# One kernel, one address: the start of the shared SBUF pool moved by 128 bytes

## The chip, the cores and the metric

The kernel runs on one core of a Trainium2 chip. The metric is the device time of one execution in microseconds. The kernel before was timed in three runs: 1452.28, 1457.98 and 1458.26 us, median 1457.98 us. A smaller number is better.

## The reference

The program computes three transformer-like layers on 256 tokens of width 1024, in float32. The first layer has a recurrent branch and an attention branch side by side; the next two have feed-forward, a mixer, a second feed-forward and a gated embedding.

```python
def reference(x, c, positions, ..., p_2, positions_2, norm_g_2, ffn1_w_in_2, ...):
    x = first_block(x, c, positions, ...)     # modulated norm, RG-LRU branch + windowed attention
    return second_block(x, p_2, positions_2, ...)

# second_block, for each of two layers i:
h = h + 0.5 * rmsnorm(swiglu(rmsnorm(h, g[0]), ffn1_w_in[i], ffn1_w_out[i]), g[1])
mix = even_mixer(...) if i % 2 == 0 else odd_mixer(...)   # HGRN2 + window attention, or retention
h = h + rmsnorm(mix, g[3])
h = h + 0.5 * rmsnorm(swiglu(rmsnorm(h, g[4]), ffn2_w_in[i], ffn2_w_out[i]), g[5])
gate = sigmoid(h @ ple_w_gate[i])
h = h + rmsnorm(gate * (p[i] @ ple_w_proj[i]), g[6])
```

`swiglu` is `(silu(x @ w_gate) * (x @ w_up)) @ w_out` with a hidden width of 2816.

## The kernel before

All weights come from HBM as "units" of 1 MB, 2048 float32 numbers on each of 128 partitions. Queue SP loads them into a ring of four (`raw`). For each unit ScalarE makes a rounded copy `whi` (L418) and VectorE the remainder `wlo = raw - whi` (L1181). The activations are split in the same way into a high and a low part. A product is then three matmuls in float32r (L2011 to L2013): high by `whi`, high by `wlo`, low by `whi`. The activations are the stationary operand (the loaded weights of the array, 128x128), the unit is the moving one (512 columns as a rule).

The 256 tokens are two tiles `t` of 128. In each stage TensorE goes through the units of the stage for t = 0 and then for t = 1; `acc[t]` in PSUM takes the sums; ScalarE and VectorE evacuate them, TensorE turns the results (L2064) and the other two engines split them again for the next stage. The order on each engine is written out by hand; semaphores hold it together. Nothing in it depends on an address.

SBUF is laid out by hand too. `sb` puts a tensor at the running offset `base[0]`, rounded up to 32 bytes (L124 to L128); `placed` puts one at a given offset (L121). Offsets are the same on all partitions. First comes what lives all the time: `raw`, `whi`, `wlo`, `h`, `xn`, `feed_hi`, `feed_lo`, gains, small tensors, `setup` and the constants. The constants of the odd layer (`decay`, `onorm_c`, L188 to L189) lie over those of the even layer and end at byte 153824. Behind them begins the pool, at `pool_at` (L190): four overlapping layouts, one each for the first layer (L193), the feed-forwards with `hid_hi` and `hid_lo` (L231), the even mixer (L241) and the odd mixer (L275). One tensor of 8 KB, `pp1` (with `fT`, `ff` and `pT0` over it), is hung from the upper end of SBUF instead (L232).

The offsets of the kernel before, in bytes and modulo 256, in the program as it is built:

| tensors | offset | mod 256 |
|---|---|---|
| `raw`, `whi`, `wlo` | 1152, 33920, 66688 | 128 |
| `h`, `xn`, `feed_hi`, `feed_lo`, `gpre`, `gpost` | 99456 to 136320 | 128 |
| `ident` (in `setup`) | 145120 | 224 |
| `decay`, `onorm_c`, `bias_b`, `mask_a`, `reset_a` | 145632 on | 224 |
| `ident_r`, `bias_r` | 150304, 150816 | 32 |
| the pool's start: `qT`, `qcT`, `feed2_hi`, `ang`, `pp0` | 153984 | 128 |
| `kT`, `hid_hi`, `mod_more`, `v1`, `mod_part`, `sz`, `hid_lo`, `hid`, `ymix`, `vc`, `sgc`, `att_c`, `red` | in the pool | 128 |
| `trn` | in the pool | 0 |
| `xc`, `rg`, `ig`, `w_ax`, `s1`, `gate_part`, `ones` | in the pool | 192 |
| `pp1`, `fT`, `ff`, `pT0` | 221056 on | 128 |

`cos_t` is at 0 and `sin_t` at 128 modulo 256; both are outside the pool.

Of the kernel before, what the change touches and what calls it, by code (L numbers as in the profile page):

```python
# [26 lines left out]
P = 128  # L27
# [22 lines left out]
C_HEADS, C_DK, C_DV = 4, 256, 512  # L50
# [63 lines left out]
def build(nc, io):  # L114
    with ExitStack() as ctx:
# [5 lines left out]
        def placed(name, shape, dtype, at):  # L121
            return nc.alloc_sbuf_tensor_at(name, shape, dtype, offset=at)
# [56 lines left out]
        const_at = base[0]  # L179
# [7 lines left out]
        bias_r = sb("bias_r", [P, 3 * P], F32R)  # L187
        decay = placed("decay", [P, C_HEADS, 3 * P], F32, const_at)  # L188
        onorm_c = placed("onorm_c", [P, C_DV], F32, const_at + 4 * C_HEADS * 3 * P)  # L189
        pool_at = (const_at + 4 * (C_HEADS * 3 * P + C_DV) + 127) // 256 * 256 + P  # L190


        base[0] = pool_at  # L193
# [2540 lines left out]
```

## Time and profile before

| | |
|---|---|
| median of three runs | 1457.98 us |
| the profiled execution's own time | 1452.28 us |
| its span | 1450.3 us |
| TensorE busy (matmul) | 1413.8 us, 97% |
| VectorE, ScalarE busy | 870.2 us, 60%; 717.3 us, 49% |
| granted TensorE clock, mean | 0.998 |
| DMA, mean | 188 GB/s |

The span is what the profiler saw of the program's instructions, and lies 2.0 us under the execution's own time. A matmul's end in the trace is modelled, so the mean duration of one (some 390 ns) is longer than the distance from one start to the next; the pace of TensorE is read from the starts in the timeline.

### The profile page before, as it was taken

How to read it: one execution, taken by the hardware profiler on the slowest of the kernel's cores; microseconds unless marked ns; L12 is line 12 of the kernel's file. 1: busy time of each engine (PE TensorE's matmuls, PEld its weight loads, DVE VectorE, ACT ScalarE, POOL GpSimd, SP SyncE). 2: the span in 40 equal slices, each digit the busy share in tenths (PEclk: the TensorE clock that was granted, in tenths of full speed). 3: DMA queues.
4: the chain of work that ended last, by engine and by line, in shares of the span. 5: the costliest groups of instructions: out<-in, count | busy, mean ns of one | idle time of the engine just before them, and what ended most of it. 6: DMA issues, size and time to landing. Idle time of an engine off the chain costs nothing.

```text
span 1450.3 us, 17117 instructions
## 1 busy us (share of the span) xinstructions
PE 1413.8 (97%) x6598; PEld 1169.5 (81%) x6598; DVE 870.2 (60%) x810; ACT 717.3 (49%) x728; POOL 80.1 (6%) x91
## 2 busy tenths in 40 slices
PE   7999999999999999999999999999999999999997
PEld 6787887777888887878888878888888878888886
DVE  7768686685554575765554575554674545654536
ACT  5674667454443456654443463543443545453434
POOL 0000000010000100110000020000202101100001
PEclk9999999999999999999999999999999999999999
DMA  9745645465646373336454655554554543644551
GB/s 394 288 147 213 221 135 185 149 221 207 230 157 219 127 258 117 145 131 231 151 200 172 228 207 203 185 194 180 195 203 146 200 148 120 243 176 172 192 186 44
DMA packets 40380, 272.51 MB, mean 188 GB/s; under 512 B 4609, under 2 KB 5505, under 8 KB 8706
## 3 DMA queue, kind: packets, MB, share of 16 engines
q1 hardware_dynamic: 36864, 261.65, 49.6%
q10 hardware_dynamic: 3458, 10.04, 2.2%
q8 instruction: 42, 0.69, 0.2%
q14 instruction: 16, 0.13, 0.0%
HBM read 270.62 MB, written 1.05 MB: 187 GB/s over the span
## 4 chain that ended last, share of the span: by engine, by line
PE 86%; DVE 9%; ACT 3%; issue 2%; POOL 0%; DMA 0%; DVEq 0%; POOLq 0%; ACTq 0%
PE acc L2011 26%; PE acc L2013 26%; PE acc L2012 26%; DVE wlo L1181 3%; PE turn L2064 3%; DVE xn L1235 1%; DVE h L1251 1%; PE turn L2213 0%; DVE feed_lo L1219 0%; PE aux L2548 0%; ACT whi L418 0%; PE aux L2139 0%; DVE mod_part L1331 0%; DVE xn L1244 0%; DVE red L1311 0%
## 5 line engine op out<-in xcount | busy, mean ns | idle before, releaser
L1181 DVE TENSOR_TENSOR wlo<-raw,whi 128x2048 fp32r<-128x2048 f32 x233 | 533.1, 2298 | 268.7 <-ACT whi L418 268.4
L2011 PE MATMUL acc<-whi,feed_hi 128*128 128x512 f32 (+1 forms) x1496 | 595.5, 398 | 9.1 <-DVE wlo L1181 7.6
L2013 PE MATMUL acc<-whi,feed_lo 128*128 128x512 f32 (+1 forms) x1496 | 583.1, 390 | 0.0
L2012 PE MATMUL acc<-wlo,feed_hi 128*128 128x512 f32 (+1 forms) x1496 | 582.6, 389 | 0.0
L418 ACT ACTIVATE whi<-raw 128x2048 fp32r<-128x2048 f32 x233 | 445.6, 1917 | 254.7 <-PE acc L2013 243.4
L2011 PEld LDWEIGHTS acc<-whi,feed_hi 128*128 128x128 f32 x1496 | 282.0, 188 | 68.9 <-DVE wlo L1181 9.6
L2013 PEld LDWEIGHTS acc<-whi,feed_lo 128*128 128x128 f32 x1496 | 281.8, 188 | 59.8
L2012 PEld LDWEIGHTS acc<-wlo,feed_hi 128*128 128x128 f32 x1496 | 282.2, 189 | 55.9 <-issue 1.2
L2011 PE MATMUL acc<-whi,hid_hi 128*128 128x512 f32 x352 | 138.0, 392 | 0.0
L2013 PE MATMUL acc<-whi,hid_lo 128*128 128x512 f32 x352 | 137.1, 389 | 0.0
L2012 PE MATMUL acc<-wlo,hid_hi 128*128 128x512 f32 x352 | 137.0, 389 | 0.0
L2013 PEld LDWEIGHTS acc<-whi,hid_lo 128*128 128x128 f32 x352 | 66.1, 188 | 13.7
L2012 PEld LDWEIGHTS acc<-wlo,hid_hi 128*128 128x128 f32 x352 | 66.1, 188 | 13.4
L2011 PEld LDWEIGHTS acc<-whi,hid_hi 128*128 128x128 f32 x352 | 66.1, 188 | 13.3
L675 ACT ACTIVATE hid_hi<-turn 128x512 f32 (+2 forms) x48 | 26.4, 549 | 99.3 <-PE turn L2064 99.3
L1654 DVE TENSOR_TENSOR hid_lo<-turn,hid_hi 128x512 f32 (+2 forms) x48 | 30.8, 642 | 71.5 <-ACT hid_hi L675 71.5
L1081 POOL TENSOR_SCALAR ms<-ss 128x1 f32<-128x1 f32 x18 | 14.3, 795 | 1062.6 <-ACT xn L438 1042.9
L1645 DVE SCALAR_TENSOR_TENSOR hid<-acc,pre_rs,sgl 128x512 f32<-128x512 f32 (+1 forms) x48 | 33.8, 703 | 46.2 <-ACT sgl L668 42.3
L1219 DVE TENSOR_TENSOR feed_lo<-turn,feed_hi 128x512 fp32r<-128x512 f32 x48 | 31.0, 686 | 35.2 <-ACT feed_hi L460 35.1
L460 ACT ACTIVATE feed_hi<-turn 128x512 fp32r<-128x512 f32 x48 | 26.2, 593 | 51.4 <-PE turn L2064 51.4
L668 ACT ACTIVATE sgl<-acc,pre_rs 128x512 f32<-128x512 f32 x40 | 27.1, 678 | 37.7 <-PE acc L2013 37.6
L2064 PE MATMUL turn<-setup,xn 128*128 128x128 f32 x250 | 34.8, 279 | 6.1 <-DVE xn L1235 6.1
(325 smaller groups left out, 862.9 us busy)
## 6 DMA issues: line engine op xcount, KB each, us to landing
raw<-in_units SPq DMA_DIRECT2D x237, 1024.0 KB, 4.9
mod_raw<-in_units SPq DMA_DIRECT2D x6, 1024.0 KB, 11.6
gpost<-in_norm_g ACTq DMA_DIRECT2D x8, 512.0 KB, 4.5
gpre<-in_norm_g ACTq DMA_DIRECT2D x6, 512.0 KB, 6.1
mod_more<-in_units SPq DMA_DIRECT2D x2, 1024.0 KB, 23.8
h<-in_x SPq DMA_DIRECT2D x2, 512.0 KB, 8.8
w_ax<-in_w_ax SPq DMA_DIRECT2D x1, 1024.0 KB, 25.7
bgate<-in_b_gate SPq DMA_DIRECT2D x1, 1024.0 KB, 27.1
```

The source lines that it names most:

```text
L418: act.activation(whi[:, u % RING, :], raw[:, u % RING, :], ACT.Copy).then_inc(hi_ready, 1)
L460: act.activation(dst[:, 4 * i:4 * i + 4, lanes(t)], turn[:, b, :].rearrange("p (c s) -> p c s", c=4), ACT.Copy).then_inc(fed_hi, 1)
L668: act.activation(sgl[:, t, :, :], acc[t][:, :].rearrange("p (i n) -> p i n", i=2)[:, :, 0:256], ACT.Silu, scale=pre_rs[:, t:t + 1]).then_i ...
L675: act.activation(dst, turn[:, b, 0:P * count].rearrange("p (c s) -> p c s", c=count), ACT.Copy).then_inc(fed_hi, 1)
L1181: dve.tensor_tensor(wlo[:, u % RING, :], raw[:, u % RING, :], whi[:, u % RING, :].bitcast(F32), ALU.subtract).then_inc(lo_ready, 1)
L1219: dve.tensor_tensor(dst[part], turn[:, b, :].rearrange("p (c s) -> p c s", c=4), hi_part[part].bitcast(F32), ALU.subtract).then_inc(moved[ ...
L1645: dve.scalar_tensor_tensor(hid[:, t, 0:tiles, :], up, pre_rs[:, t:t + 1], sgl[:, t, 0:tiles, :], ALU.mult, ALU.mult)\
L1654: dve.tensor_tensor(hid_lo[:, at, lanes(t)], turn[:, b, 0:P * count].rearrange("p (c s) -> p c s", c=count), hid_hi[:, at, lanes(t)].bitca ...
L2011: pe.matmul(out, xh, wh, start=first, stop=False)
L2012: pe.matmul(out, xh, wl, start=False, stop=False)
L2013: return pe.matmul(out, xl, wh, start=False, stop=last)
L2064: last = pe.transpose(turn[:, b, P * i:P * i + P], part, ident[:, :])
```

## The change

The expression for the start of the pool is another one.

```diff
--- before.py
+++ after.py
@@ -187,7 +187,7 @@
         bias_r = sb("bias_r", [P, 3 * P], F32R)
         decay = placed("decay", [P, C_HEADS, 3 * P], F32, const_at)
         onorm_c = placed("onorm_c", [P, C_DV], F32, const_at + 4 * C_HEADS * 3 * P)
-        pool_at = (const_at + 4 * (C_HEADS * 3 * P + C_DV) + 127) // 256 * 256 + P
+        pool_at = (const_at + 4 * (C_HEADS * 3 * P + C_DV) + 127) // 128 * 128
 
 
         base[0] = pool_at
```

With the constants' end at 153824, the old expression gives 153951 // 256 * 256 + 128 = 153984, the new one 153951 // 128 * 128 = 153856. Each tensor of the pool lies 128 bytes lower than before: those at 128 modulo 256 come to 0, those at 192 to 64, `trn` from 0 to 128. `pp1` and its overlays stay, and so does all that stands ahead of the pool. No instruction is added, removed or moved on any engine or queue, and no shape changes.

## Rows read from the trace of the kernel before

**Rows 1.** The page: busy time by engine, and the chain that ended last

```profile
PE 1413.8 (97%) x6598; PEld 1169.5 (81%) x6598; DVE 870.2 (60%) x810; ACT 717.3 (49%) x728; POOL 80.1 (6%) x91
PE 86%; DVE 9%; ACT 3%; issue 2%; POOL 0%; DMA 0%; DVEq 0%; POOLq 0%; ACTq 0%
PE acc L2011 26%; PE acc L2013 26%; PE acc L2012 26%; DVE wlo L1181 3%; PE turn L2064 3%; DVE xn L1235 1%; DVE h L1251 1%; PE turn L2213 0%; DVE feed_lo L1219 0%; PE aux L2548 0%; ACT whi L418 0%; PE aux L2139 0%; DVE mod_part L1331 0%; DVE xn L1244 0%; DVE red L1311 0%
```

**Rows 2.** Waits of TensorE: us in total, times, longest us

```profile
PE aux L2128 <- DMA mod_raw<-in_units: 8.3, 1, 8.3
PE acc L2011 <- DVE wlo L1181: 7.6, 6, 2.6
PE turn L2064 <- DVE xn L1235: 6.1, 7, 1.8
PE aux L2139 <- DVE mod_part L1334: 2.5, 1, 2.5
```

**Rows 3.** Timeline of TensorE in the second feed-forward matrix: start us, us, instruction

```profile
469.65 0.39 PE L2012 MATMUL acc<-wlo,hid_hi 128*128 128x512 f32 x1
...
472.37 0.39 PE L2012 MATMUL acc<-wlo,hid_hi 128*128 128x512 f32 x1
```

**Rows 4.** The same where `feed_hi` is the stationary operand

```profile
603.71 0.39 PE L2011 MATMUL acc<-whi,feed_hi 128*128 128x512 f32 x1
...
605.53 0.40 PE L2013 MATMUL acc<-whi,feed_lo 128*128 128x512 f32 x1
```

**Rows 5.** The same at the narrow unit of the even mixer, 256 columns

```profile
514.63 0.28 PE L2012 MATMUL acc<-wlo,feed_hi 128*128 128x256 f32 x1
...
515.35 0.28 PE L2012 MATMUL acc<-wlo,feed_hi 128*128 128x256 f32 x1
```

**Rows 6.** The same early in a deep group, with a longer step

```profile
451.26 0.40 PE L2013 MATMUL acc<-whi,hid_lo 128*128 128x512 f32 x1
451.50 0.39 PE L2011 MATMUL acc<-whi,hid_hi 128*128 128x512 f32 x1
451.72 0.40 PE L2012 MATMUL acc<-wlo,hid_hi 128*128 128x512 f32 x1
```

**Rows 7.** Groups by form, TensorE: busy us, mean ns of one, idle before

```profile
L2011 PE MATMUL acc<-whi,hid_hi 128*128 128x512 f32 x352 | 138.0, 392 | 0.0
L2213 PE MATMUL turn<-xc,w_ax 128*128 128x256 f32 x32 | 7.6, 381 | 0.4 <-DVE qT L1208 0.4
L2226 PE MATMUL aux<-kT,qT 128*128 128x256 f32 x16 | 4.8, 380 | 0.0
L2548 PE MATMUL aux<-vc,att_c 128*128 128x512 f32 x16 | 7.9, 593 | 0.0
L2273 PE MATMUL aux<-gate_part,ones 128*128 128x512 f32 x4 | 1.9, 592 | 0.0
...
L2012 PEld LDWEIGHTS acc<-wlo,hid_hi 128*128 128x128 f32 x352 | 66.1, 188 | 13.4
```

**Rows 8.** Groups by form, VectorE

```profile
L1307 DVE TENSOR_SCALAR trn<-trn 128x352 f32<-128x352 f32 x2 | 0.7, 344 | 0.1
L1315 DVE TENSOR_SCALAR red<-red 128x352 f32<-128x352 f32 x1 | 0.3, 344 | 0.0
L1535 DVE TENSOR_TENSOR sz<-sz,xc 128x1024 f32<-128x1024 f32 x2 | 2.5, 1226 | 0.3
L1505 DVE TENSOR_TENSOR ig<-ig,xc 128x1024 f32<-128x1024 f32 x2 | 2.4, 1216 | 0.0
L1461 DVE TENSOR_TENSOR h<-h,xn 128x1024 f32<-128x1024 f32 x2 | 2.5, 1226 | 0.1
```

**Rows 9.** The start: DMA issues (KB each, us to landing), ScalarE's wait, one window

```profile
mod_more<-in_units SPq DMA_DIRECT2D x2, 1024.0 KB, 23.8
ACT whi L418 <- DMA raw<-in_units: 7.4, 3, 5.3
20.00:40.00 20.00, 20.00 (x93) 17.77 (x93) 14.87 (x15) 12.57 (x15) 0.00 (x0) 1.00 1.01 419
```

## The prediction

> **What bounds the kernel now.** I read the busy shares first, then the chain that ended last, then TensorE's waits, and then the starts of its matmuls one by one. TensorE is busy for 97% of the span, and the chain runs through it for 86% [rows 1]; 78% of the span is the three lines of the split product. What TensorE waits for is short: the four largest entries are 8.3, 7.6, 6.1 and 2.5 us, 24.5 us together [rows 2], and the two of them that don't belong to the start are 13.7 us. So there are two ways in which a change of address can move the time: another pace of the matmuls, or another duration of one of the few instructions of VectorE and ScalarE (and of the loads at the start) that the chain passes through.
>
> The pace is read from starts. In the second feed-forward matrix twelve steps lie between 469.65 and 472.37 us [rows 3], which is 226.7 ns a matmul. With `feed_hi` as the stationary operand eight steps lie between 603.71 and 605.53 [rows 4], 227.5 ns. With 256 columns in place of 512, six steps take 0.72 us [rows 5], 120 ns. The difference, 106.7 ns for 256 columns, is 0.417 ns a column, so 512 columns are 213.3 ns, and 13.3 ns in each matmul are a fixed part. TensorE keeps this pace for as long as it isn't made to wait: it is the bound, and nothing in it looks like a queue for SBUF.
>
> **The change, part by part.** No instruction comes, goes or changes its place or its shape, so there is no removed or added work to sum. What changes is the address of operands. By arithmetic the pool goes from 153984 to 153856, a move of 128 bytes, and from 128 to 0 modulo 256. It is a real move, so the case "the new expression gives the same address" is out. The constants below it end at 153824 and the nearest tensor above, `pp1`, stays, so nothing overlaps anew and no semaphore gets another meaning. I take the operands engine by engine.
>
> 1. TensorE. The moving operand of the split product (`whi`, `wlo`) stays where it is. The stationary one moves in three places: `hid_hi` and `hid_lo` in the four feed-forwards, 3 x 352 = 1056 matmuls (one of the three groups of 352 stands in [rows 7]; the other two have the same count); `feed2_hi` and `feed2_lo` in one group of the odd mixer, 4 units by 2 tiles by 12 matmuls = 96 by the code; `pT1` in one projection of the embedding, 24 (one unit, 2 tiles by 4 blocks by 3). That is 1176 matmuls. The trace has no matmul with an operand at 0 modulo 256, so their new pace isn't shown; what it shows are the neighbours. At 192 modulo 256 (`xc`, `w_ax`) a matmul of 256 columns is 381 ns, at 128 (`kT`, `qT`) 380 ns; with `gate_part` and `ones`, both at 192, one of 512 columns is 592 ns, with `vc` and `att_c`, at 128, 593 ns [rows 7]. Two different addresses of this kind differ by 1 ns in 380 to 590. I take 0 for the move. The bounds: above, the longer step that sometimes appears even now, 0.24 us between 451.26 and 451.50 against 0.22 to 0.23 around it [rows 6]; with the hundredths of the view that is up to some 9 ns over the usual step, and if all 1176 matmuls had it the sum is 1176 x 9 = 10.6 us. Below, the fixed part: if the loading of an aligned operand hid all of the 13.3 ns, the gain were 1176 x 13.3 = 15.7 us.
>
> 2. VectorE and ScalarE. Here the trace does have both alignments. The same operation on 352 elements takes 344 ns where `trn` is at 0 modulo 256 and 344 ns where `red` is at 128 [rows 8]. An addition or product of 1024 elements takes 1226 ns with one operand at 128 and the other at 192, 1226 ns with both at 128 (`h`, `xn`), and 1216 ns with both at 192. So the largest difference is 10 ns in 1226, 0.8%, and it is not tied to the pool's edge. The chain has 9% of VectorE and 3% of ScalarE [rows 1]; less the 3% for `wlo`, whose operands don't move, 9% of 1450.3 us are 131 us. With all of it changed by 0.8% that is 1.0 us in either direction. I take 0. Off the chain these engines have 40% and 51% of the span to spare, so there is cover for any such difference; if it were gone, this 1.0 us is what it costs.
>
> 3. DMA. The transfers into the pool all come at the start, apart from one `pT` load and a one-row bias. Between 20 and 40 us the DMA share is 1.01 at 419 GB/s, and ScalarE waits 7.4 us for units in this part of the program [rows 9]. So the start does depend on transfers, and `mod_more`, two transfers of 1 MB, stands in the queue ahead of the units that ScalarE waits for. At 419 GB/s the two are 2 x 1.05 MB / 419 = 5.0 us of the queue. The ring's own rows of the same size go to addresses at 128 modulo 256 now, and will still; no row of this trace has a transfer of that size to an address at 0, so I bound it by a tenth of these 5.0 us either way, 0.5 us, and take 0.
>
> A rule of the Trainium skill bears on this last term. The page "DMA: Bandwidth & Descriptors", section "How a descriptor splits into AXI transactions", says that a transfer is cut into pieces of 256 B which must begin at a multiple of 256, so that a misaligned one pays for a further piece. By it, read as holding for the destination too, a row of 8192 B of `mod_more` needs 33 pieces now and 32 after the change, 3% less: an estimate by that page of 0.15 us gained in 5.0 us. No run here has shown it yet, and the ring's 237 loads wouldn't gain, since they stay where they are.
>
> The sum is 0 us, with -15.7 - 1.0 - 0.5 and 10.6 + 1.0 + 0.5 as its outer bounds. Against the profiled execution's own 1452.28 us (its span 1450.3 and 2.0 around it) that is 1452.3 again. The two other runs of the kernel before are at 1457.98 and 1458.26, so the profiled one is the fast end of the scatter; the mean of the three is 1456.2 and their median 1458.0. A median of some runs of an unchanged kernel should fall between them: I forecast 1457.0 us.
>
> **The rivals.**
>
> Slower: the two reads of TensorE get into each other's way. Now the stationary and the moving operand both begin at 128 modulo 256; after the change the stationary one of 1176 matmuls begins at 0 and the moving one still at 128. If SBUF served reads that begin in the same half of 256 bytes better than others, each of these matmuls would get a longer step. Its place is the feed-forwards; its price by [rows 6] is up to 9 ns each, 10.6 us, so 1467.6 us. It decides by more than 0.5% from 6.2 ns a matmul on (7.3 us / 1176). For it: steps of 0.24 us do occur in the trace with no change of work. Against it: in [rows 7] neither `w_ax` nor `ones` at another alignment costs anything. The Trainium skill, page "SBUF — State Buffer", section "Who interferes with whom", speaks against it as well: TensorE has one read port for the moving operand and an independent one for the loading, and never waits. The steady 226.7 ns agree with that, but a run with the two operands apart isn't among the rows.
>
> Faster: the aligned stationary operand loads faster, and a part of the fixed 13.3 ns goes. The full price is 15.7 us, which gives 1441.3; half of it, 7.8 us, gives 1449.2. For it: there is a fixed part, and nothing in the trace has an operand at 0, so it can't be excluded. Against it: at 192 and at 128 modulo 256 it is the same, and a load takes 188 ns [rows 7] against a step of 227, beside the matmul before, so it seems to be covered.
>
> Also possible is a shift of the evacuations or of the start (points 2 and 3), by at most 1.5 us together in either direction. It stays within the forecast, whatever its sign.
>
> **How the numbers follow.** About 0.5%, 7.3 us, is what a measurement of this kernel can tell from no change. I give the forecast (no change, the small shifts included) 0.64, the slower case 0.20, and the faster one 0.16. The last two aren't smaller because the one alignment that the change brings is just the one that TensorE's rows don't show. The scatter of the runs before, 6 us, is under the half per cent. The likeliest case alone would span 1451 to 1461. The range reaches to the slower case's full price at 1468, and towards the faster one to 1445, something over its half price: 1445 to 1468. Faster 0.16, same 0.64, slower 0.20.
>
> **What would show it right or wrong.** Right: in the profile after, the starts in the second feed-forward matrix are again 227 ns apart, as are those with `feed_hi`; VectorE's groups of the same form agree within 10 ns; the waits of TensorE are the same few, within 2 us. The slower rival shows as a step over 227 ns with `hid_hi` and `hid_lo` and not with `feed_hi`; the faster one as a step under 227 there. The start is judged by ScalarE's wait for units, 7.4 us now. The forecast is wrong if the medians of both kernels, run side by side, lie over 0.5% apart, and wrong in its reasons if any group whose operands moved has another mean while the total happens to agree.

## The result, and the profile after

The kernel after takes 1463.82 us (median of 12 runs, 1459.42 to 1465.99) against 1455.43 us for the kernel before in the same comparison (12 runs, 1452.28 to 1458.26). The ratio is 1.0055, with a 95% interval of 1.0044 to 1.0066: slower, by 8 us, through an address alone. Not one instruction is another.

The page of the profile after, busy time and then the chain, against [rows 1]:

```profile
span 1462.6 us, 17117 instructions
PE 1426.6 (98%) x6598; PEld 1175.2 (80%) x6598; DVE 870.2 (59%) x810; ACT 717.7 (49%) x728; POOL 79.2 (5%) x91
PE 87%; DVE 9%; ACT 3%; issue 1%; POOL 0%; DMA 0%; DVEq 0%; POOLq 0%; ACTq 0%
```

The span is 12.3 us longer and TensorE is busy 12.8 us longer; VectorE and ScalarE have the same busy time to within 0.4 us. The waits of TensorE after (us in total, times, longest) are those of [rows 2]:

```profile
PE aux L2128 <- DMA mod_raw<-in_units: 8.0, 1, 8.0
PE acc L2011 <- DVE wlo L1181: 7.3, 5, 2.6
PE turn L2064 <- DVE xn L1235: 6.2, 7, 1.8
PE aux L2139 <- DVE mod_part L1334: 2.8, 1, 2.8
```

So the time is not in a wait that the profile knows. It is in the pace, the distance from the start of one matmul to the start of the next (a step). In the second matrix of the first feed-forward 180 matmuls with `hid_hi` and `hid_lo` stand in a row. I take the last 168 of them, 167 steps, in both kernels. Timeline of before (start us, us, instruction; `...` stands for lines left out):

```profile
461.95 0.39 PE L2011 MATMUL acc<-whi,hid_hi 128*128 128x512 f32 x1
...
499.80 0.39 PE L2013 MATMUL acc<-whi,hid_lo 128*128 128x512 f32 x1
```

and of after:

```profile
464.23 0.39 PE L2011 MATMUL acc<-whi,hid_hi 128*128 128x512 f32 x1
...
480.26 0.40 PE L2011 MATMUL acc<-whi,hid_hi 128*128 128x512 f32 x1
480.50 0.39 PE L2012 MATMUL acc<-wlo,hid_hi 128*128 128x512 f32 x1
...
503.04 0.39 PE L2013 MATMUL acc<-whi,hid_lo 128*128 128x512 f32 x1
```

37.85 us / 167 = 226.7 ns before, 38.81 / 167 = 232.4 ns after. The three other feed-forwards give the same two numbers to 0.02 ns, worked out from the unrounded starts. Before, every step is 226 or 227 ns; after, they run 228, 230, 233, 241, 232, 231, 232 and round again, whether VectorE and ScalarE are busy at the time or not. The duration that the profile prints for a matmul shows it less exactly: this group went from 392 ns [rows 7] to 398, the two others with `hid` from 389 to 394, and that with `whi` and `feed_hi`, of which at most 32 in 1480 have an operand that moved, from 399 to 401.

```profile
L2011 PE MATMUL acc<-whi,hid_hi 128*128 128x512 f32 x352 | 140.0, 398 | 0.0
L2213 PE MATMUL turn<-xc,w_ax 128*128 128x256 f32 x32 | 7.6, 381 | 0.4 <-DVE qT L1208 0.4
L2548 PE MATMUL aux<-vc,att_c 128*128 128x512 f32 x16 | 7.9, 593 | 0.0
L2273 PE MATMUL aux<-gate_part,ones 128*128 128x512 f32 x4 | 1.9, 592 | 0.0
```

The other rows of that group moved too, from 192 to 64 or from 128 to 0 modulo 256, and are unchanged to the nanosecond.

Summed over all starts, the steps that follow a `hid` matmul are 5.8 us longer than before, those of the 96 with `feed2` 0.55 us, and those of the 24 with `pT1` 0.12 us: 6.5 us. The remaining 5.8 us between the two spans (that it is the same number is chance) lie in stretches in which one of the two executions was granted the lower clock. Three stretches of after, us, busy times, then granted clock, DMA share, GB/s:

```profile
328.40:331.90 3.50, 3.50 (x11) 2.88 (x11) 1.38 (x2) 1.20 (x2) 0.00 (x0) 0.51 0.72 186
632.20:635.70 3.50, 3.17 (x10) 2.68 (x11) 1.66 (x3) 2.25 (x5) 0.21 (x2) 0.51 0.02 5
860.90:867.80 6.90, 6.02 (x14) 4.75 (x15) 2.03 (x3) 0.48 (x2) 1.43 (x2) 0.51 0.87 345
```

and the place of the first in before:

```profile
327.90:331.40 3.50, 3.50 (x20) 2.87 (x19) 1.55 (x3) 1.20 (x2) 0.07 (x1) 1.00 0.54 166
```

In the three the clock is at its lower level, 1.2 GHz, and the first holds 11 matmuls where the same 3.5 us of before hold 20. These stretches come and go from one execution to the next in both kernels, so I compare executions of equal mean clock, over all that are on record for the two kernels. The median span is 1457.8 us against 1450.5 at the clock 0.998 (2 executions of after, 6 of before), 1460.1 against 1453.9 at 0.996 (5 and 20), and 1462.0 against 1455.3 at 0.994 (4 and 8): 7.3, 6.2 and 6.7 us. That is the change, and it is the 6.5 us counted in the steps above to within 0.8 us.

The other 2 us or so of the 8.4 between the medians go with a lower clock: 11 of the 23 executions of after are at 0.993 or 0.992, and none of the 40 of before. Whether the address does that isn't shown. The kernel with the ring moved, below, has the same longer steps and ran at 0.994 to 0.996, in four executions.

### The profile page after: what moved, and what is told of

Same layout as the page of the kernel before. It is cut to its first block, busy times and chain, and to the rows that moved or that the text cites. A ratio compares the mean times of both kernels' runs of the same rounds, so it can differ in the third digit from the quotient of the medians.

```text
span 1462.6 us, 17117 instructions
## 1 busy us (share of the span) xinstructions
PE 1426.6 (98%) x6598; PEld 1175.2 (80%) x6598; DVE 870.2 (59%) x810; ACT 717.7 (49%) x728; POOL 79.2 (5%) x91
## 4 chain that ended last, share of the span: by engine, by line
PE 87%; DVE 9%; ACT 3%; issue 1%; POOL 0%; DMA 0%; DVEq 0%; POOLq 0%; ACTq 0%
PE acc L2011 26%; PE acc L2013 26%; PE acc L2012 26%; PE turn L2064 4%; DVE wlo L1181 3%; DVE xn L1235 1%; PE turn L2213 0%; DVE feed_lo L1219 0%; PE aux L2548 0%; DVE h L1251 0%; PE aux L2139 0%; DVE mod_part L1331 0%; DVE red L1311 0%; DVE xn L1244 0%; ACT whi L418 0%
## 5 line engine op out<-in xcount | busy, mean ns | idle before, releaser
L1081 POOL TENSOR_SCALAR ms<-ss 128x1 f32<-128x1 f32 x18 | 13.3, 740 | 1074.6 <-ACT xn L438 1054.7
## 6 DMA issues: line engine op xcount, KB each, us to landing
mod_more<-in_units SPq DMA_DIRECT2D x2, 1024.0 KB, 23.5
```

## The experiments

I had one theory to test from here, A: a matmul's step gets longer where the stationary operand and the moving one stand at different places modulo some power of two. The rivals stand in each expectation. Two operands are called in step where they start at the same place modulo 256, and out of step otherwise. All kernels start from the kernel before, and the cuts of code are shortened. Where a table gives the step, it is that over the last 168 matmuls of the stage, as above.

**Put `hid` back, and move everything else in the pool.**

```diff
-        pool_at = (const_at + 4 * (C_HEADS * 3 * P + C_DV) + 127) // 256 * 256 + P
+        pool_at = 153856
-        hid_hi = sb("hid_hi", ...); hid_lo = sb("hid_lo", ...)
+        # both placed 128 bytes higher than sb would
```

> The pool starts at 153856 as after the change, but hid_hi and hid_lo alone are put back to 128 modulo 256. Theory A (a matmul step gets longer where the stationary operand and the moving one begin in different halves of 256 bytes): the steps with hid_hi and hid_lo are 227 ns again, 6 us of the 8 come back, and the median is at most 0.1% over that of before; the 96 matmuls with feed2 and the 24 with pT1 keep their longer step, 0.6 us. Rival B (the loss is in the granted clock and in other tensors of the pool): hid's steps are 227 ns but the time stays about 0.5% over before. Rival C (the trace's longer steps come from something that follows the pool's start as such): hid's steps stay at 232.9 ns.

1457.25 us (11 runs), ratio to before 1.0006 (0.9997 to 1.0015). Timeline of this kernel:

```profile
464.46 0.39 PE L2017 MATMUL acc<-whi,hid_hi 128*128 128x512 f32 x1
...
502.31 0.39 PE L2019 MATMUL acc<-whi,hid_lo 128*128 128x512 f32 x1
```

226.7 ns again. The two `hid` tensors carry the loss: all other tensors of the pool together are worth at most 0.15%, the upper end of the interval, and that includes the 0.6 us of `feed2` and `pT1`. Rival B, the clock or the rest of the pool, and rival C fall.

**Move the ring instead of the pool.**

```diff
-        base = [(nc.sbuf_usable_end - nc.sbuf_bytes_remaining + 31) // 32 * 32]
+        base = [(nc.sbuf_usable_end - nc.sbuf_bytes_remaining + 31) // 32 * 32 + 128]
...
+        pool_at = 153984     # the value that before has
```

> All tensors ahead of the pool (raw, whi, wlo, h, xn, feed_hi, feed_lo, constants) move up by 128 bytes to 0 modulo 256, and the pool stays at 153984, 128 modulo 256. Theory A, as a matter of the distance between the two operands: hid's steps are 232.9 ns, feed's 227, time 0.5% over before, as after the change. Rival A2, as a matter of the stationary operand's own address (0 modulo 256 is bad): hid's steps are 227, those of feed_hi and feed_lo 232.9, 4392 x 5.7 ns = 25 us more than before, 1.7%. Rival A3 (a moving operand at 0 modulo 256 is bad or good by itself): all steps change alike.

1462.04 us (4 runs), ratio 1.0043 (1.0027 to 1.0058).

```profile
462.56 0.39 PE L2011 MATMUL acc<-whi,hid_hi 128*128 128x512 f32 x1
...
501.37 0.39 PE L2013 MATMUL acc<-whi,hid_lo 128*128 128x512 f32 x1
```

`hid` hasn't moved here; `whi` and `wlo` have, and the step is 232.4 ns, while those with `feed_hi` and `feed_lo`, which moved along with the ring, keep 227. It is the distance between the operands, not the address of either.

**Ring and pool at 0 modulo 256.** The same with `pool_at = 154112`. `pp1` and what lies over it, hung from the upper end, stay at 128.

> Everything ahead of the pool at 0 modulo 256 (moved up by 128) and the pool at 154112, 0 modulo 256 as well. Distance theory: hid's and feed's steps are all 227 ns and the time is that of before, ratio 0.998 to 1.002. Rival (an operand of TensorE at 0 modulo 256 costs or gains by itself): steps other than 227 in both groups.

1456.04 us (10 runs), ratio 1.0001 (0.9991 to 1.0012).

```profile
463.04 0.39 PE L2011 MATMUL acc<-whi,hid_hi 128*128 128x512 f32 x1
...
500.89 0.39 PE L2013 MATMUL acc<-whi,hid_lo 128*128 128x512 f32 x1
```

37.85 us again, so 226.7 ns, as in the three other stages; 156 matmuls with `feed_hi` and `feed_lo` in a row step at 227.3 ns here and before. This closes the square: ring and pool at (128, 128) and (0, 0) are alike, (128, 0) and (0, 128) are both slower.

**Put the other operand out of step.** `base[0] += 128` ahead of `feed_hi`, `pool_at = 153984`.

> feed_hi and feed_lo, and the gains and constants behind them, move up by 128 bytes; raw, whi, wlo and the pool stay. The suspected cost is put on the other 4392 matmuls of the split product. Theory A: their steps are 232 to 233 ns in place of 227, 4392 x 5.7 = 25 us more, a ratio of 1.017 to before, less where TensorE waits anyway; hid's steps stay at 227. Rival (the effect belongs to hid's stage: no turns in between, addresses in the high part of SBUF): feed's steps stay at 227 and the time is that of before.

1473.23 us (4 runs), ratio 1.0114 (1.0098 to 1.0129). A stage of 156 matmuls with `feed_hi` and `feed_lo`, before:

```profile
1111.80 0.48 PE L2011 MATMUL acc<-whi,feed_hi 128*128 128x512 f32 x1
...
1147.03 0.39 PE L2013 MATMUL acc<-whi,feed_lo 128*128 128x512 f32 x1
```

and here:

```profile
1130.51 0.48 PE L2012 MATMUL acc<-whi,feed_hi 128*128 128x512 f32 x1
...
1166.61 0.40 PE L2014 MATMUL acc<-whi,feed_lo 128*128 128x512 f32 x1
```

35.23 / 155 = 227.3 ns against 36.10 / 155 = 232.9, while the steps with `hid` are at 226.7 again. The effect follows the operands, in this stage as in that of `hid`. Its size was expected at 25 us and came to 17 us between the medians. At equal mean clock the spans are 20 us apart at 0.998 (1470.8 against 1450.5) and 17 at 0.997 (1469.4 against 1452.3), from one or two executions each. Over the whole kernel the mean step with `feed` rose from some 227.6 to 232.8 ns, 5.2 and not 5.7, which makes 23 us. A part of the rest is in TensorE's waits, which are shorter in this profile: 6.1 us in place of 7.6 for `wlo` and 5.0 in place of 6.1 for `xn`, with 9.5 in place of 8.3 for `mod_raw` against them.

One group of `feed` shows no loss: the 48 matmuls of 256 columns in the even mixer. Here, out of step,

```profile
523.83 0.28 PE L2012 MATMUL acc<-whi,feed_hi 128*128 128x256 f32 x1
...
526.57 0.28 PE L2014 MATMUL acc<-whi,feed_lo 128*128 128x256 f32 x1
```

23 steps take 2.74 us, 119 ns each, against 120 before [rows 5]. So the 5.7 ns are shown for 512 columns alone.

**Which load, and which distance.** From here each feed-forward has its own pair of `hid` tensors at its own offset, four distances in one run:

```diff
+        hid_his = [placed(f"hid_hi{k}", [P, FF_CHUNKS, SEQ], F32R, hid_at + d)
+                   for k, d in enumerate((128, 0, 64, 32))]
+        hid_los = [placed(f"hid_lo{k}", [P, FF_CHUNKS, SEQ], F32R, hid_at + hid_size + d)
+                   for k, d in enumerate((0, 128, 64, 32))]
```

> The pool as before; in each of the four feed-forwards hid_hi and hid_lo lie somewhere else: in the first hid_hi is 128 bytes off and hid_lo in place, in the second the other way round, in the third both 64 bytes off, in the fourth both 32. Theory A, each load paying for its own distance to the moving operand: the mean step over a stage of 180 is 226.7 + 2/3 x 5.7 = 230.5 ns in the first and 228.6 in the second; in the third and fourth it says nothing yet: equal to 232.9 if any distance but a multiple of 256 costs, 227 if only the half of 256 bytes counts and 32 and 64 leave both in one half, in between if it grows with distance. Rival (one disturbed step upsets all that follow): 232.9 in the first and in the second.

```profile
465.50 0.39 PE L2017 MATMUL acc<-whi,hid_hi 128*128 128x512 f32 x1
...
504.46 0.39 PE L2019 MATMUL acc<-whi,hid_lo 128*128 128x512 f32 x1
...
780.30 0.39 PE L2017 MATMUL acc<-whi,hid_hi 128*128 128x512 f32 x1
...
818.90 0.40 PE L2019 MATMUL acc<-whi,hid_lo 128*128 128x512 f32 x1
...
997.55 0.39 PE L2017 MATMUL acc<-whi,hid_hi 128*128 128x512 f32 x1
...
1036.51 0.39 PE L2019 MATMUL acc<-whi,hid_lo 128*128 128x512 f32 x1
```

One run, 1463.61 us. 38.96, 38.60 and 38.96 us for 167 steps: 233.3, 231.1 and 233.3 ns, and 233.3 in the fourth. Two misses. A load out of step does not simply pay its third: `hid_hi` alone out of step (233.3) is worse than both (232.4), and `hid_lo` alone costs 4.4 ns, over two thirds of the full price. And the half of 256 bytes isn't the unit: 32 bytes off cost as much as 64.

**More distances.** (96, 192, 224, 256), then (160, 288, 384, 512), the same for both tensors.

> Both hid tensors off by 96, 192, 224 and 256 bytes in the four feed-forwards; all else as before. If only a distance of a multiple of 256 is in step: 233 to 234 ns in the first three stages and 227 in the last. If only the order matters (the load a little behind the moving operand costs, a little ahead doesn't): 227 at 224 as well. If it is the exact old address that counts: the last stage is slow too.

> Both hid tensors off by 160, 288, 384 and 512 bytes in the four feed-forwards. If what counts is the distance modulo 256: the step at 288 is that at 32, 233.3 ns, at 384 that at 128, 232.4 ns, at 512 that at 0 and 256, 226.7 ns; 160 is new and lies somewhere over 226.7. If the period is longer than 256 (512 or more), 288 and 384 give other steps than 32 and 128.

One run each, 1461.3 and 1460.6 us; the second stood beside one run of before of 1455.99. Of the first of these two kernels, at 192 and 256 bytes:

```profile
781.02 0.39 PE L2017 MATMUL acc<-whi,hid_hi 128*128 128x512 f32 x1
...
819.25 0.39 PE L2019 MATMUL acc<-whi,hid_lo 128*128 128x512 f32 x1
...
1385.03 0.39 PE L2017 MATMUL acc<-whi,hid_hi 128*128 128x512 f32 x1
...
1422.88 0.39 PE L2019 MATMUL acc<-whi,hid_lo 128*128 128x512 f32 x1
```

Of the second, at 384 and 512 bytes:

```profile
996.62 0.40 PE L2017 MATMUL acc<-whi,hid_hi 128*128 128x512 f32 x1
...
1035.42 0.39 PE L2019 MATMUL acc<-whi,hid_lo 128*128 128x512 f32 x1
...
1384.23 0.39 PE L2017 MATMUL acc<-whi,hid_hi 128*128 128x512 f32 x1
...
1422.09 0.39 PE L2019 MATMUL acc<-whi,hid_lo 128*128 128x512 f32 x1
```

| distance of `hid` from the ring, modulo 256 | 0 | 32 | 64 | 96 | 128 | 160 | 192 | 224 |
|---|---|---|---|---|---|---|---|---|
| step, ns | 226.7 | 233.3 | 233.3 | 234.3 | 232.4 | 233.3 | 228.9 | 233.3 |
| seen again at +256 | 226.7 (256, 512) | 233.3 (288) | | | 232.4 (384) | | | |

The period is 256 bytes, as the second of these runs was expected to show to a tenth of a nanosecond. Of the distances tried, only the multiples of 256 are free; 192 costs 2.2 ns, the rest 5.7 to 7.6.

**Take `wlo` out of step with `whi`.**

```diff
+        base[0] += 128
         wlo = sb("wlo", [P, RING, UNIT], F32R)
+        base[0] += 128
...
-        pool_at = (const_at + 4 * (C_HEADS * 3 * P + C_DV) + 127) // 256 * 256 + P
+        pool_at = 154240
+        # hid_hi 0, 0, 128, 128 and hid_lo 0, 128, 0, 128 bytes on; mod_raw's second half placed at wlo
```

> wlo alone is moved to 0 modulo 256; whi, feed_hi, feed_lo stay at 128. hid_hi and hid_lo lie, in the four feed-forwards in turn, at (128, 128), (128, 0), (0, 128) and (0, 0) modulo 256. From the run in which the two were moved by themselves: 231.6 ns if the one load of hid_lo is out of step, 233.8 if the two of hid_hi are, 232.9 if all three are, 227 if none is. Theory D (a load must be in step with the moving operand that streams while it runs, that of the matmul before): one, none, three, two loads out of step, so some 231.6, 227, 232.9, 233.8 ns. Theory O (it must be in step with the moving operand of its own matmul): one, two, one, two: 231 to 234 in every stage, the second included. Theory M (the two moving operands must be in step with each other, whatever the loads do): none of the four at 227. The matmuls with feed_hi and feed_lo have one load out of step under D as under O, so the whole is slower than before by some 1.0 to 1.4%.

1475.5 us, one run. Stages two and three:

```profile
786.98 0.40 PE L2020 MATMUL acc<-whi,hid_hi 128*128 128x512 f32 x1
...
825.58 0.39 PE L2022 MATMUL acc<-whi,hid_lo 128*128 128x512 f32 x1
...
1004.53 0.39 PE L2020 MATMUL acc<-whi,hid_hi 128*128 128x512 f32 x1
...
1042.76 0.39 PE L2022 MATMUL acc<-whi,hid_lo 128*128 128x512 f32 x1
```

The steps are 231.1, 231.1, 228.9 and 228.9 ns in the four stages. Theory D (each load in step with the operand that streams meanwhile) wanted some 227 in the second, and O (in step with the operand of its own matmul) wanted 231 to 234 in every stage, where the third and fourth are at 228.9; both fall as they were put. Theory M gave only that none is at 226.7, and that holds, but it gives no size. The 156 matmuls with `feed` in a row, arranged as `hid` is in the first stage, step at 231.6 ns, and the whole is 1.3% over the median of before, as expected. With the earlier runs, all eight ways to put `hid_hi`, `hid_lo` and `wlo` either at `whi`'s place modulo 256 or 128 bytes off it are measured, and one alone is free: all in step.

**The identity.** `base[0] += 160` ahead of `setup` brings the identity of the turns from 224 to 128 modulo 256.

> Setup and all constants move up by 160 bytes, so that the identity of the 530 turns is at 128 modulo 256 like the operand it meets; the pool and the ring stay where they were before the change. In the profile before, the eleven steps that follow a turn take 2604 ns at the median, 110 ns more than eleven of 226.7. If that settling comes from the identity's address, 88 of these places give back up to 110 ns each, 9 us or 0.6%, and this is faster than before. If it comes from the change of kind of matmul, nothing changes: ratio 1.000.

1455.09 us (12 runs), ratio 0.9993 (0.9983 to 1.0003): no difference that can be told. The eleven steps after a turn take 2610 ns at the median, 2604 before. Their settling isn't due to the identity's address. The turns, matmuls of 128 columns, follow each other at 109 ns at the median in both, with their operands 96 bytes apart modulo 256 before and in step here.

## Why the prediction was wrong

The forecast was no change, and the sign was missed. That 1463.8 us lies inside the range is no merit of the reasoning: the range took its upper end from the slower rival's full price. And the 6.8 us between it and the forecast of 1457.0 are less than the change, because before came out at 1455.4. The slower rival, which had 0.20, gave the right sign, the right place and a price that holds as a bound. Its own condition, reads in the same half of 256 bytes, isn't what counts: 32 and 64 bytes apart leave both operands in one half and cost 6.6 ns.

- **What bounds the kernel**: right. All of the loss is on TensorE, and none in a wait.
- **Point 1, "I take 0 for the move"**: this step failed. The four rows that I set beside each other [rows 7] showed matmuls at 192 and at 128 modulo 256 to be alike, and I read that as "the address doesn't matter". But `xc` and `w_ax` are both at 192, `kT` and `qT` both at 128, `gate_part` and `ones` both at 192, `vc` and `att_c` both at 128. In each row the distance between the two operands is a multiple of 256, so they all show the one case that is free. The rows couldn't speak on the case that the change makes, operands 128 bytes apart, and I used them against it nevertheless. The measured term is 5.7 ns a step, 6.5 us over the 1176 matmuls; the bound from [rows 6], 9 ns and 10.6 us, held. By these steps alone the change would be 0.45%, under the 0.5% from which the prediction counted it as one; the medians lie 0.55% apart, with the lower clock of after in them. The trace of before did hold operands apart, in the turns (the identity at 224, `xn` and `hid` at 128), but these have 128 columns and show no difference.
- **The faster rival**, a part of the fixed 13.3 ns gone with an operand at 0 modulo 256: no. With both operands at 0 the step is 226.7 ns.
- **Point 2, VectorE and ScalarE**: right. `trn` and `red` changed places between 0 and 128 modulo 256; the rows of after answer to [rows 8] within 2 ns:

```profile
L1307 DVE TENSOR_SCALAR trn<-trn 128x352 f32<-128x352 f32 x2 | 0.7, 345 | 0.1
L1315 DVE TENSOR_SCALAR red<-red 128x352 f32<-128x352 f32 x1 | 0.3, 343 | 0.0
L1535 DVE TENSOR_TENSOR sz<-sz,xc 128x1024 f32<-128x1024 f32 x2 | 2.5, 1226 | 0.3
L1505 DVE TENSOR_TENSOR ig<-ig,xc 128x1024 f32<-128x1024 f32 x2 | 2.4, 1218 | 0.0
```

- **Point 3, DMA**: right as far as it can be seen. `mod_more` lands after 23.5 us in place of 23.8, and ScalarE's wait for units at the start is 7.4 us as in [rows 9]. An effect of 0.15 us can't be told from nothing here.
- **The page "SBUF — State Buffer" of the Trainium skill**, section "Who interferes with whom", gives TensorE two independent read ports and says that it never waits. I used it against the slower rival. Here the measurements differ: with 128 bytes between the operands each step is 5.7 ns longer, and the measurement decides. They don't show that the two reads collide; they show only that the pace depends on the distance, at 512 columns.
- **How the measurement scatters**: the 6 us from run to run that I took as noise are mostly the stretches at the lower clock. In before the median span goes from 1450.5 us at the clock 0.998 to 1455.3 at 0.994. Comparing executions of equal mean clock gives 6.2 to 7.3 us for the change, where the medians give 8.4.

What stays open is the mechanism below the rule: why `hid_hi` alone out of step is worse than both, why 192 bytes cost least, and why moving `wlo` off makes the step with both `hid` tensors off shorter (228.9 in place of 232.4). What in the chip has the period of 256 bytes, and why 256 columns show no loss, isn't shown by any run here.

## What to carry to other kernels

Where a kernel is bound by a steady chain of float32r matmuls of 512 columns whose weights are reloaded each time, place both operands of TensorE, and each of several moving tensors, a multiple of 256 bytes apart in the partition; here every other multiple of 32 cost 1.0 to 3.4% of the pace. Read the pace from the starts of matmuls; the printed durations rest on modelled ends, and a group's mean takes in the clock as well. Compare executions of equal mean clock where the effect is as small as the scatter. And when rows of a trace are to bound a case that it doesn't contain, ask what all of them have in common: four rows that agree may be one case, four times.

## What was new of the hardware

A float32r matmul of 512 columns with a reload before it steps at 226.7 ns when its operands are a multiple of 256 bytes apart, and at 228.9 to 234.3 ns otherwise, at 128 bytes in a fixed pattern of seven steps between 228 and 241 ns that is the same in all four feed-forwards. At 256 columns the same distance of 128 bytes leaves the step at 119 to 120 ns. An instruction of VectorE at another offset modulo 256 is unchanged within 2 ns in 1226. Apart from the very end, the granted clock falls to its lower level for 3.4 or 6.8 us at a few places of an execution, and which places differs between executions. In the profile of after they begin at 116.9, 328.5, 632.3 and 861.0 us, and idle times of TensorE of 2.6, 1.8, 1.4 and 0.7 us ended 0.7 to 1.4 us before; before has the first alone, at 116.2 us, though its other waits are much the same.
